# Second MLP matrix by Strassen's scheme, residual with tokens on partitions, layers written out

## What is computed

```
u = rms_norm(x, norm1_w[l])            # projections of u, three branches, gates
x = x + mixed @ w_o[l]                 # [512,1024] @ [1024,1024]
h = rms_norm(x, norm2_w[l])
x = x + square(relu(h @ w_up[l])) @ w_down[l]   # [1024,4096], then [4096,1024]
```

## Time and profile before

| | |
|---|---|
| median of 3 runs | 1655.81 us (1655.64 to 1656.78) |
| the profiled execution | 1654.38 us, its span 1652.6 us |
| TensorE matmul busy | 1617.4 us (98%), 7656 matmuls |
| VectorE busy | 926.8 us (56%) |
| ScalarE busy | 628.0 us (38%) |
| mean granted TensorE clock | 0.997 |
| DMA | 150.92 MB, 28.3% of 16 engines |

### The profile page before, as it was taken

One profiled execution on the slowest core, in us unless ns is written; L12 is line 12 of the kernel. 1 busy time (PEld: TensorE's weight loads), 2 busy tenths in 40 slices (PEclk: granted clock), 3 DMA queues, 4 the chain that ended last, 5 costly groups with the idle time before them and its releaser, 6 DMA issues.

```text
span 1652.6 us, 22309 instructions
## 1 busy us (share of the span) xinstructions
PE 1617.4 (98%) x7656; PEld 1326.4 (80%) x7656; DVE 926.8 (56%) x1365; ACT 628.0 (38%) x1000; POOL 0.2 (0%) x4
## 2 busy tenths in 40 slices
PE   5999999999999999999999999999999999999997
PEld 4877778888888888888887777888888888888886
DVE  5576675455565444454656667654456544445456
ACT  5446652233343142323435566432234322323242
POOL 0000000000000000000000000000000000000000
PEclk9999999999999999999999999999999999999999
DMA  4331123233333223332322212133223332333221
GB/s 145 103 102 52 52 82 98 77 102 102 102 102 100 92 89 102 102 102 80 102 82 99 77 52 78 52 108 122 77 76 128 101 99 82 102 102 102 85 93 51
DMA packets 135659, 150.92 MB, mean 91 GB/s; under 512 B 4848, under 2 KB 122128, under 8 KB 135568
## 3 DMA queue, kind: packets, MB, share of 16 engines
q1 hardware_dynamic: 135136, 149.69, 28.3%
q10 hardware_dynamic: 432, 0.08, 0.0%
HBM read 147.67 MB, written 2.10 MB: 91 GB/s over the span
## 4 chain that ended last, share of the span: by engine, by line
PE 95%; DVE 2%; ACT 1%; DVEq 1%; DMA 0%; issue 0%; ACTq 0%; SPq 0%
PE acc L454 27%; PE acc L455 27%; PE acc L456 27%; PE acc L485 3%; PE acc L487 3%; PE acc L486 3%; PE bank L639 1%; PE bank L658 1%; PE bank L650 1%; PE bank L597 1%; PE bank L611 0%; DMA x_tokens<-in_x_dram 0%; DVE x_tokens L1342 0%; PE bank L570 0%; PE bank L586 0%
## 5 line engine op out<-in xcount | busy, mean ns | idle before, releaser
L454 PE MATMUL acc<-uh,wh 128*128 128x512 f32 x1152 | 454.8, 395 | 8.8 <-DVE wl L951 7.6
L456 PE MATMUL acc<-uh,wl 128*128 128x512 f32 x1152 | 449.9, 391 | 0.0
L455 PE MATMUL acc<-ul,wh 128*128 128x512 f32 x1152 | 449.9, 391 | 0.0
L742 ACT ACTIVATE wh<-raw 128x1024 fp32r<-128x1024 f32 x227 | 238.8, 1053 | 280.9 <-PE acc L456 269.0
L454 PE MATMUL acc<-yh,wh 128*128 128x512 f32 (+1 forms) x832 | 324.4, 390 | 0.6 <-DVE yl L1263 0.6
L455 PE MATMUL acc<-yl,wh 128*128 128x512 f32 (+1 forms) x832 | 324.2, 390 | 0.0
L456 PE MATMUL acc<-yh,wl 128*128 128x512 f32 (+1 forms) x832 | 324.2, 390 | 0.0
L951 DVE TENSOR_TENSOR wl<-raw,wh 128x1024 fp32r<-128x1024 f32 x227 | 278.0, 1225 | 48.5 <-ACT wh L742 30.5
L454 PEld LDWEIGHTS acc<-uh,wh 128*128 128x128 f32 x1152 | 216.8, 188 | 59.8 <-issue 14.5
L456 PEld LDWEIGHTS acc<-uh,wl 128*128 128x128 f32 x1152 | 216.7, 188 | 45.7
L455 PEld LDWEIGHTS acc<-ul,wh 128*128 128x128 f32 x1152 | 217.0, 188 | 43.5
(11 more groups left out here) (182 smaller groups left out, 1237.2 us busy)
## 6 DMA issues: line engine op xcount, KB each, us to landing
raw<-in_w_in_dram SPq DMA_DIRECT2D x40, 1024.0 KB, 5.2
raw<-in_w_up_dram SPq DMA_DIRECT2D x32, 1024.0 KB, 5.3
raw<-in_w_down_dram SPq DMA_DIRECT2D x32, 1024.0 KB, 5.0
raw_branch<-in_w_in_dram SPq DMA_DIRECT2D x12, 1024.0 KB, 4.9
raw_branch<-in_w_branch_dram SPq DMA_DIRECT2D x12, 1024.0 KB, 5.0
raw<-in_w_o_dram SPq DMA_DIRECT2D x8, 1024.0 KB, 5.0
x_tokens<-in_x_dram SPq DMA_DIRECT2D x4, 512.0 KB, 5.5
raw_kv<-in_w_in_dram SPq DMA_DIRECT2D x4, 512.0 KB, 3.8
```

Source lines behind the costliest of these rows:

```text
L454: nc.tensor.matmul(acc[b][:], h[:, k, :], right_h(k), start=k == 0, stop=False)
L455: nc.tensor.matmul(acc[b][:], h[:, k, :], right_l(k), start=False, stop=False)
L456: return nc.tensor.matmul(acc[b][:], lo[:, k, :], right_h(k), start=False, stop=k == n - 1)
L742: nc.scalar.activation(split_view(True, base, pos), raw_view(base, pos), ACT.Copy).then_inc(hi_done, 1)
```

## The change

- **Second matrix.** In each quarter the product [512 tokens x 1024 hidden] by [1024 x 1024] is cut 2 x 2 and done in seven products of [256 x 512] by [512 x 512] (Strassen's scheme in Winograd's form). A product is two units `dn` (a pair, one half of its contraction each), each of 2 token tiles x 2 rows x 3 = 12 matmuls: 168 a quarter, where there were 192. Tokens lie on the output's partitions; the weights are the moving operand.
- **What the scheme needs.** VectorE makes four sums of weight blocks for each of the two halves in place in the loaded block (`weight_sum`, 128x1024 each), two while `up6` and `up7` run, two in the places j = 2 and 3 of the second matrix. It also makes three sums of 256 columns for each of four hidden tiles and one difference of 128x1024 (`hidden_low`), and all get a high part from ScalarE and a low part from VectorE. ReLU and square are both ScalarE's now. Four product sums are kept in SBUF over the quarters; only in the last one are they scaled into the residual (`down_result`).
- **Residual.** `x_tok` with tokens on partitions throughout. `w_o` is done by tokens. The normed operand is made from TensorE transposes of `x_tok` (fills `V0` to `V7` before the MLP, `UT0` to `UT7` before a layer), ScalarE and VectorE reading them from PSUM. Norm sums are ScalarE squares with accumulation, so the matmuls with ones, the row broadcast for the MLP and the transposes at the end are gone. The result is stored straight from `x_tok`, in eight pieces.
- **Order.** The projection tables are re-arranged (first `gq` and `gk` by halves, the second half of the contraction first); all loops over layers and quarters are written out. `w_down` comes in four transfers of 1 MB a quarter into two buffers of their own, issued by SyncE behind the quarter's four slabs of `w_up`.

```diff
-                def mlp_quarter(q, first=False, final=False):
...
-                        else:
-                            k = pos - 8
-                            a, free = done(l, M0, q, pos)
-                            V.tensor_tensor(T[2], a[:], rs2[:], ALU.mult).then_inc(free, 1)
-                            V.drain()
-                            V.tensor_tensor(xT[:, k, :], xT[:, k, :], T[2], ALU.add)
...
+                def hidden_low(n, i):
+
+                    V.drain()
+                    if i < BK:
+                        dve.wait_ge(hid_hi, 8 * n + i + 1)
+                        V.tensor_tensor(h11[1][:, i, :], hid[:, i, 0:2 * P], h11[0][:, i, :].bitcast(f32),
+                                        ALU.subtract).then_inc(hid_ready, 1)
+                        if i == BK - 1:
+                            V.tensor_tensor(hd_sum[:], hid[:, 0:BK, 0:2 * P], hid[:, 0:BK, 2 * P:],
+                                            ALU.subtract).then_inc(diff_val, 1)
+                    else:
+                        k = i - BK
+                        dve.wait_ge(hid_val, 8 * n + i + 1)
+                        s1, s2, s4 = (hs_sum[:, k, z, :] for z in range(3))
+                        V.tensor_tensor(s1, hid[:, k, 2 * P:], hid[:, i, 2 * P:], ALU.add)
+                        V.drain()
+                        V.tensor_tensor(s2, s1, hid[:, k, 0:2 * P], ALU.subtract)
+                        V.drain()
+                        V.tensor_tensor(s4, hid[:, i, 0:2 * P], s2, ALU.subtract).then_inc(sums_val, 1)
+                        V.drain()
+                        dve.wait_ge(hid_hi, 8 * n + i + 1)
+                        V.tensor_tensor(h2[1][:, k, :], hid[:, i, :], h2[0][:, k, :].bitcast(f32),
+                                        ALU.subtract).then_inc(hid_ready, 1)
...
+                    for t in range(2):
+                        a, free = tile_ready(dve, l, f"p{7 * q + i}", t)
+                        g1, g6, g5, g7 = (g[:, t, :] for g in gsum)
+                        if i in (1, 5, 6):
+                            row, half = {1: (0, 0), 5: (0, 1), 6: (1, 0)}[i]
+                            scaled_into_x(2 * row + t, half, a[:]).then_inc(free, 1)
...
+                                V.tensor_tensor(g, g, a[:], ALU.add).then_inc(free, 1)
+                        if not final:
+                            continue
+                        V.drain()
+                        if i == 0:
+                            scaled_into_x(t, 0, g1)
+                            V.tensor_tensor(g6, g6, g1, ALU.add)
...
+                for q in range(QUARTERS):
...
+                    for i in range(8):
+                        V.drain()
+                        split_ahead(l, f"up{8 * q + i}")
...
+                        if i >= 6:
+                            weight_sum(b12[i - 6], b22[i - 6], b12[i - 6], ALU.subtract)
+                            weight_sum(b11[i - 6], b12[i - 6], b11[i - 6], ALU.add).then_inc(weights_summed, 1)
+                        if i:
+                            hidden_low(n, i - 1)
...
+                        if i > BK + 1:
+                            sums_low(n, i - BK - 2)
+                    for j in range(PRODUCTS * PAIRS):
+                        V.drain()
+                        if j == 0:
+                            hidden_low(n, KT - 1)
+                            sums_low(n, BK - 2)
+                            sums_low(n, BK - 1)
+                        if j in (2, 3):
+                            weight_sum(b21[j - 2], b21[j - 2], b11[j - 2], ALU.subtract)
+                            weight_sum(b11[j - 2], b22[j - 2], b11[j - 2], ALU.subtract).then_inc(weights_summed, 1)
+                        if j % 2 == 0 and j:
+                            down_result(q, j // 2 - 1)
+                        split_ahead(l, f"dn{14 * q + j}")
```

On ScalarE the list of a `w_up` unit is now: split ahead, then, once the unit has ended, relu, square, high copy, and from the sixth unit on the high copy of the sums (`hidden_sums_high`):

```diff
+                        split_ahead(l, f"up{8 * q + i}")
...
+                        a, free = done(act, l, f"up{8 * q + i}")
+                        nc.scalar.activation(hid[:, i, :], a[:], ACT.Relu).then_inc(free, 1)
+                        nc.scalar.drain()
+                        nc.scalar.activation(hid[:, i, :], hid[:, i, :], ACT.Square).then_inc(hid_val, 1)
+                        nc.scalar.drain()
...
+                        if i > BK:
+                            hidden_sums_high(n, i - BK - 1)
```

More of the change, by code:

```diff
@@ new lines, with add_fills @@
+ACC_USE, ACC_USES = {}, [0] * 4
+for _key, _banks in ACC_BANKS.items():
+    for _b in _banks:
+        ACC_USES[_b] += 1
+        ACC_USE[_key, _b] = ACC_USES[_b]
+TILE_OF = {}
+for _key, _banks in ACC_BANKS.items():
+    if len(_banks) > 1:
+        TILE_OF[_key] = sum(len(ACC_BANKS[k]) - 1 for k in TILE_OF)
+TILES = sum(len(ACC_BANKS[k]) - 1 for k in TILE_OF)
+FILL = {}
+def add_fills(layer, words):
+    for word in words:
+        FILL[layer, word] = len(FILL)
+add_fills(0, [f"UT{k}" for k in range(KT // 2, KT)])
@@ L427, in _ @@
+            for n in range(2 * TT):
+                t, half = ((0, 0), (1, 0), (2, 1), (3, 1), (0, 1), (1, 1), (2, 0), (3, 0))[n]
+                sp.wait_ge(x_upd, 16 * (DEPTH - 1) + 8 + n + 1)
+                cols = slice(half * SEQ, (half + 1) * SEQ)
+                sp.dma_start(out[0, t * P:(t + 1) * P, cols], x_tok[:, t, cols]).then_inc(out_full, 16)
+            sp.wait_ge(out_full, 16 * 2 * TT)
         @block.tensor
@@ L463, in unit @@
+            def unit(l, u, right, pieces=(0, 1), ready=None, ready_at=None, gate=None, back=False):
+                n, slot, a = k_tiles(u), UNIT[u] % SPLIT, acc[ACC_BANKS[u][0]]
+                order = [(k + n // 2) % n if back else k for k in range(n)]
+                if 0 in pieces:
+                    pe.wait_ge(lo_done, unit_at(l, u) + 1)
+                    open_acc(l, u)
                 if gate is not None:
                     gate()
[L465 removed]
+                for at_k in range(n // 2 * pieces[0], n // 2 * (pieces[-1] + 1)):
+                    k = order[at_k]
@@ L1335, in _ @@
-                mlp_quarter(0, first=True)
-                with dve.Fori(1, QUARTERS - 1) as q:
-                    mlp_quarter(q)
-                mlp_quarter(QUARTERS - 1, final=True)
-            for e in range(2 * TT):
-                t, half = e // 2, e % 2
-                dve.wait_ge(bank_full, DEPTH * N_FILLS + XF + e + 1)
-                V.tensor_copy(x_tok[:, t, half * 512:(half + 1) * 512], bank[e % 4][:]).then_inc(bank_free[e % 4], 1)
-                V.drain().then_inc(out_copied, 1)
+                                if i % 4:
+                                    mixed_low(i % 8 - 1)
@@ new lines, in _, with residual @@
+                                split_ahead(l, f"br{i}")
+                mixed_low(KT - 1)
+                for pair in range(PAIRS):
+                    V.drain().then_inc(down_free[pair], 1)
+                def residual(key, t, half):
+                    a, free = tile_ready(dve, l, key, t)
+                    x_at = x_tok[:, t, half * SEQ:(half + 1) * SEQ]
+                    V.tensor_tensor(x_at, a[:], x_at, ALU.add).then_inc(free, 1)
+                    V.drain().then_inc(x_upd, 1)
```

975 lines of the change are left out of this document (497 added, 478 removed).

## The result

| | before | after |
|---|---|---|
| median | 1656.30 us (1655.64 to 1656.96, 4 runs) | 1688.05 us (1687.93 to 1688.50, 4 runs) |
| the profiled execution, its span | 1654.38, 1652.6 us | 1687.93, 1686.1 us |

The ratio is 1.0192 with a 95% interval of 1.0175 to 1.0210: the change makes the kernel 1.9% slower. The forecast was 1687 us, 31 us above the kernel before.

What follows compares the result with a forecast made beforehand. The kernel was taken as bound by its number of matmuls. Terms -43.5 + 78.2 + 10.5 - 3.3 - 3.5 - 9.0 + 1.7 = +31.1 on 1654.4 gave 1685.5, plus 1.4 for the median: 1687 us, range 1652 to 1706.

Steps and rivals of the forecast that it cites:

- Matmuls, -43.5: In the second matrix 24 of 192 matmuls go from each of 8 quarters, at 0.227 us each: 43.5 us less.
- VectorE's waits, +78.2: TensorE waits for VectorE's list: 7.3 us per ordinary quarter, 15.6 and 18.9 in last quarters; 78.2 us together.
- my reading of the signs: TensorE idle some 80 us, nearly all before products; VectorE busy over 90% from `up6` to `dn3`.
- My own step about the clock: In ordinary quarters slow matmuls after a wait cost nothing, only filling the 2.8 us of waits behind.
- Transposes, +10.5: New transposes of `x_tok`, 64 before the MLPs and 32 before layer 2, at 0.87 us per 8: 10.5 us more.
- Clock, +1.7: Before layer 2 nothing fills the loss from the lower clock after a wait: 1.7 us more.
- Start -3.5, end -9.0, norm sums -3.3: First matmul earlier, -3.5 us with a norm sum; shorter tail after the last matmul, -9.0; norm sums and row broadcasts gone, -3.3.
- the third and fourth rival: Clock loss not absorbed after 4.5 us waits, 1701 us, 12%; queued 1 MB loads, 1698 us, 4%.
- VectorE keeping up: Rival: in the second matrix VectorE keeps pace and every wait goes, 1607 us; 6%.
- Free drains: Rival: a VectorE drain costs nothing next to other work, waits shrink to 35 us in all, 1644 us; 8%.
- The clock: Rival: every wait of 4.5 us costs 1.7 us through the lower clock, 14 us more, 1701 us; 12%.
- Late loads: Rival: 1 MB transfers queue, 5 MB at 5.0 us each, costing 1 to 2 us a quarter, 1698 us; 4%.

Runs made afterwards that it cites:

- plain product: The changed kernel with eight plain units of 24 matmuls a quarter in place of Strassen's products: 1647.43 us, ratio 0.9949.
- best version: The changed kernel with ScalarE's next split first, two weight differences made earlier and a shorter last quarter: 1636.72 us; also without the 22 drains a quarter, 1627.16 us.

## Why the prediction was right

The mechanism was right. The two profiled executions are 33.5 us apart where the sum had 31.1: the waits came out 2.5 us larger, the clock's loss 1.0 larger, the end 1.1 better. The median of 1688.05 lies 1.05 above the forecast, which is closer than the sum was, by luck: I added 1.4 us for the distance of a profiled execution from the median, and this kernel's is 0.1.

- **Matmuls, -43.5.** The pitch stayed 0.227 outside the waits and the slow matmuls behind them. In the waits before `dn3` matmuls are free: the run that puts 192 there has the same time.
- **VectorE's waits, +78.2.** Ordinary quarters wait 7.7 us each, not 7.3: 46.0 for six. In layer 2 the last quarter goes from the last matmul of `dn2`, 1636.56, to the last of all, 1682.39, in 45.8 us where 132 matmuls need 29.9: 15.9 (predicted 15.6). In layer 1, up to the transposes at 849.10, it is 46.2 for 121 matmuls, 27.4: 18.8 (18.9). Together 80.7. The wait before `dn3` was 4.8 where 4.5 was predicted.
- **Where my reading of the signs was off.** I said that TensorE's idle time would rise to "some 80 us", nearly all of it in front of products. By the page it is 81.6 (35.2 before), but some 20 us of that are the start and the end, and 6.4 the projections. The waits in front of products and of the transposes for layer 2 are 43.5 + 6.0 + 4.6 and half a microsecond of small ones, 55. The other 26 are matmuls at the lower clock and pauses that the list doesn't carry. My own step about the clock implied this, and I did not carry it over to what the list would show. VectorE's share from `up6` to `dn3` is 88%, not over 90, because drains are not counted as busy.
- **Transposes, +10.5.** Right: 16 take 1.67 us until the next matmul starts, and that one lasts 0.09 more, so 1.75 with 1.74 predicted. (The 1.91 in the row counts to the modelled end of the last and overlaps what follows.)

```profile
469.18 1.91 PE L543 MATMUL bank<-consts,x_tokens 128*128 128x128 f32 x16
...
849.10 3.65 PE L543 MATMUL bank<-consts,x_tokens 128*128 128x128 f32 x16 [4.59 <-DVEq L1405]
852.40 0.78 PE L527 MATMUL acc<-wh_rows,hidden_hi 128*128 128x512 f32 x1
...
856.24 0.40 PE L478 MATMUL acc<-uh,wh 128*128 128x512 f32 x1
```

- **Clock, +1.7.** It fell where I said, but cost 2.7 us. The transposes at 849.10 and the 12 matmuls of `dn13` behind them last 7.14 us, until 856.24, where 1.75 + 2.72 were due. I took the 1.7 from the wait of 3.2 us in the earlier trace rows; this one is 4.6 us. The granted clock is 0.50 over the transposes and still 0.71 in `dn13`, and nothing behind fills the loss:

```profile
849.10:852.75 3.65, 3.65 (x17) 3.65 (x18) 3.25 (x4) 2.06 (x3) 0.00 (x0) 0.50 0.35 79
852.70:855.90 3.20, 3.20 (x12) 2.55 (x11) 2.65 (x4) 0.69 (x1) 0.00 (x0) 0.71 0.23 80
```

- **Start -3.5, end -9.0, norm sums -3.3.** The start measured -3.5, by luck to the decimal: it was an estimate with bounds 0 and 6 (and 3 with a norm sum of 0.8 makes 3.8), and the first matmul stands anywhere from 20.05 to 20.91 in the profiles of the experiments, most of it the wait for the first load. The end took 3.7 for 13.8, -10.1; one of the two adds that I had counted runs before the last matmul. The norm sums were not measured by themselves. The plain product tests these terms together, within a few us: they make +10.5 - 3.3 - 2.8 - 10.1 = -5.7 there (its first matmul stands at 20.77), and the spans differ by -4.7.
- **The sum as measured:** -43.5 + 80.7 + 10.5 + 2.7 - 3.3 - 3.5 - 10.1 = +33.5, with the matmuls and the norm sums as computed, and the spans differ by 33.5. `w_o`, loads and the projections cost nothing, as said: the only waits in the projections are those of before, twice 3.2.
- **The range.** 1652 to 1706 does not follow from its parts. Waits of 54 us with the start's bound of 6 give about 1660, and waits of 94 us with the third and fourth rival would be above 1720. The time lies inside either range.
- **The rivals.** VectorE keeping up: it doesn't in this order, and almost does in the order of the best version, where the time is below the plain product's. Free drains: 8 us were in 22 of them a quarter. The clock: absorbed before the products, not before the transposes. Late loads: the four transfers of 1 MB land in 11.1 us, not 5.0, but no wait of TensorE names them.

The addition of VectorE's list, on which the forecast rested, was 3% off. It, and in the later runs what the earlier ones had measured, gave seven of the eight runs that change the order, the work or the drains within 4 us; the one it missed was GpSimd, where it had no row for the price.

## What to carry to other kernels

A scheme that trades matmuls for additions is paid on the vector engines, and there not by their mean load: add up, in program order, what stands between the splits that the lookahead covers, and compare that with the lookahead. Halving the length of a unit (2.72 for 5.44 us) halves a lookahead counted in units. Work that depends on loads alone belongs where the engine idles, and the split that TensorE will want next belongs at the head of the list, ahead of the work for the unit that just ended; these two moves, a shorter last quarter and fewer drains turned +1.9% into -1.7%.

## What the runs showed of the hardware

- An idle GpSimd is no free adder beside VectorE: 0.42 us became 2.67 while a GpSimd sum of 128x1024 ran, though copies out of PSUM kept their 0.69.
- The lower clock behind a wait cost nothing where the engine behind which TensorE waits sets the next start too: 1.00 for 0.59 in the window, 1687.7 for 1688.0 us. Before the transposes for layer 2, where nothing follows that would absorb it, the drop behind a wait of 4.6 us cost 2.7 us.
- An explicit drain on VectorE cost 0.18 us between two operations of 1024 columns (2.53 against 2.35 us for the pair) and 0.19 between two of 512.
